# Two weight pieces over the first token half in eight banks, warm-up products, low weight parts on VectorE

## The reference, cut to what matters

```python
h = rmsnorm(x, g_mix)
z = h @ w_in                       # 1024 x 1792: lx, lg, q, k, v
lx = causal_depthwise_conv(lx, w_conv, b_conv)
y_lru = rmsnorm(rg_lru(lx, ...) * gelu(lg), g_lru_out)
y_att = rmsnorm(chunk_window_attention(q, k, v, sinks), g_attn_out)
x = x + concatenate([y_lru, y_att]) @ w_out
x = x + square(relu(rmsnorm(x, g_ffn) @ w_ff1)) @ w_ff2
x = x + sigmoid(rmsnorm(x, g_ple) @ w_ple_gate) * (p @ w_ple_proj)
return rmsnorm(x, g_final)
```

## Time and profile before

| | us |
|---|---|
| median of 3 runs (range) | 1108.56 (1108.11 to 1109.01) |
| profiled execution, its time | 1109.54 |
| its span, first to last instruction | 1107.8 |
| TensorE busy | 1073.4 (97%) |
| TensorE weight loads | 870.7 (79%) |
| VectorE busy | 726.7 (66%) |
| ScalarE busy | 419.5 (38%) |
| GpSimd busy | 472.1 (43%) |

### The profile page before, as it was taken

How to read it: one execution, slowest core, us unless ns; L and a number is a source line. 1 busy time by engine, 2 the same in 40 slices (tenths; PEclk the granted TensorE clock), 3 DMA queues, 4 the chain that set the end, 5 groups by cost and what they waited for, 6 DMA issues and landing times.

```text
span 1107.8 us, 13619 instructions
## 1 busy us (share of the span) xinstructions
PE 1073.4 (97%) x4898; PEld 870.7 (79%) x4898; DVE 726.7 (66%) x921; ACT 419.5 (38%) x725; POOL 472.1 (43%) x304
## 2 busy tenths in 40 slices
PE   6899999899999999999999999999999999999995
PEld 5778888677876888888888888888888888888895
DVE  6997666889799836536536546546545545696557
ACT  7555664454456222222222222212312312565334
POOL 2744252333306256255255355355355355293221
PEclk9999999999999999999999999999999999999998
DMA  8211102111001211211211211211111101420004
GB/s 285 77 39 38 38 1 86 39 39 39 1 1 38 76 38 38 76 38 38 76 38 38 76 38 38 76 38 40 73 38 51 63 38 61 167 76 1 1 1 153
DMA packets 20162, 61.05 MB, mean 55 GB/s; under 512 B 2080, under 2 KB 4128, under 8 KB 20128
## 3 DMA queue, kind: packets, MB, share of 16 engines
q1 hardware_dynamic: 19584, 60.08, 15.2%
q10 hardware_dynamic: 544, 0.52, 0.1%
HBM read 56.40 MB, written 4.19 MB: 55 GB/s over the span
## 4 chain that ended last, share of the span: by engine, by line
PE 79%; DVE 11%; ACT 4%; issue 3%; POOL 2%; DMA 1%; SPq 0%; DVEq 0%; ACTq 0%
PE bank L567 26%; PE bank L568 25%; PE bank L569 25%; POOL w_lo L444 1%; DVE r_mix L1288 1%; DVE lane L1335 1%; DMA stage<-in_w_in 1%; DVE acc L343 1%; POOL gx_lo L473 1%; DVE r_ffn L1288 1%; PE bank L657 1%; PE bank L615 1%; DVE xT L1682 1%; DVE h_lo L1550 1%; DVE xT L1754 1%
## 5 line engine op out<-in xcount | busy, mean ns | idle before, releaser
L567 PE MATMUL bank<-h_hi,w_hi 128*128 128x512 f32 (+1 forms) x724 | 282.6, 390 | 13.7 <-DVE h_lo L1275 9.8
L568 PE MATMUL bank<-h_lo,w_hi 128*128 128x512 f32 (+1 forms) x724 | 276.7, 382 | 0.0
L569 PE MATMUL bank<-h_hi,w_lo 128*128 128x512 f32 (+1 forms) x724 | 276.4, 382 | 0.0
L1682 DVE TENSOR_TENSOR xT<-bank,xT 128x512 f32<-128x512 f32 x256 | 173.7, 688 | 114.0 <-PE bank L569 112.3
L567 PE MATMUL bank<-u_hi,w_hi 128*128 128x512 f32 x512 | 202.2, 395 | 2.4 <-DVE xT L1682 1.1
L569 PE MATMUL bank<-u_hi,w_lo 128*128 128x512 f32 x512 | 199.4, 389 | 0.0
L568 PE MATMUL bank<-u_lo,w_hi 128*128 128x512 f32 x512 | 199.4, 389 | 0.0
L567 PEld LDWEIGHTS bank<-h_hi,w_hi 128*128 128x128 f32 x724 | 137.0, 189 | 46.6 <-issue 16.1
L521 POOL TENSOR_TENSOR w_lo<-w_raw,w_hi 128x1024 fp32r<-128x1024 f32 x30 | 78.1, 2624 | 192.2 <-ACT w_hi L1152 192.2
L568 PEld LDWEIGHTS bank<-h_lo,w_hi 128*128 128x128 f32 x724 | 137.0, 189 | 27.0 <-issue 1.9
L569 PEld LDWEIGHTS bank<-h_hi,w_lo 128*128 128x128 f32 x724 | 137.0, 189 | 26.5
(11 more groups left out here) (208 smaller groups left out, 1694.6 us busy)
## 6 DMA issues: line engine op xcount, KB each, us to landing
w_raw<-in_w_ff SPq DMA_DIRECT2D x60, 512.0 KB, 3.7
stage<-in_w_in SPq DMA_DIRECT2D x13, 512.0 KB, 3.4
stage<-in_w_out SPq DMA_DIRECT2D x8, 512.0 KB, 3.5
stage<-in_w_ple_gate SPq DMA_DIRECT2D x8, 512.0 KB, 3.9
xT<-in_x SPq DMA_DIRECT2D x7, 512.0 KB, 9.7
stage<-in_w_ff SPq DMA_DIRECT2D x4, 512.0 KB, 3.2
out_x<-xT SPq DMA_DIRECT2D x4, 512.0 KB, 2.9
out_x<-xT SPq DMA_DIRECT2D x6, 256.0 KB, 2.9
```

Source lines behind the costliest of these rows:

```text
L567: pe.matmul(o, whi, hh, start=first, stop=False, skip_group_check=onto)
L568: pe.matmul(o, whi, hl, start=False, stop=False, skip_group_check=onto)
L569: return pe.matmul(o, wlo, hh, start=False, stop=last, skip_group_check=onto)
L1682: dve.tensor_tensor(dst, bank[4 + q % 4][:, :], dst, ALU.add).then_inc(y_added, 1)
```

## The change

The first four half pieces are loaded, split and used in the order piece 0 first half, piece 1 first half, piece 0 second half, piece 1 second half (`place`). TensorE's `first_half` runs four groups (two pieces, both channel blocks) over the first half of the tokens, into banks 0 to 3; groups 4 to 7 are the same two pieces over the second half of the tokens, in banks 4 to 7 with no wait for an evacuation (`in_group`, `main_bank`). The two row sums move: the first between the third and the fourth half piece, the second into the middle of group 5. Nine products of ones with ones (`WARM`) run at the start into bank 7. Tile 0 of x is issued from ScalarE's queue. All low parts of the input projection's pieces 0 to 6 are now written by VectorE (`w_low`); GpSimd keeps the low parts of the gate inputs, the later row sums of squares and the later pieces. VectorE adds all squares of x. The gate products move to groups 8, 12, 16 and 19, and the steps tied to them with them; the row sums of the recurrent output move one group later, to 23 and 24.

```diff
-GATE_AT = [5, 9, 13, 17]
+GATE_AT = [7, 11, 15, 18]
+WARM = 9
...
             if g < L0:
-                return bank[g % IN_BANKS], g - IN_BANKS if g >= IN_BANKS else None
+                if g < 8:
+                    return bank[g], None
+                return bank[g % IN_BANKS], g - 8 if g < 12 else g - IN_BANKS
...
+        def in_group(g):
+            if g < 8:
+                return (g % 4) // 2, g // 4, g % 2
+            return g // 4, (g % 4) // 2, g % 2
+        def place(s):
+            return (s % 2, s // 2) if s < 4 else (s // 2, s % 2)
...
-            if n < IN_PIECES:
+            if n < 2:
+                eng.wait_ge(main_done, 6 + 2 * n)
+            elif n < IN_PIECES:
...
-            sp.dma_start(xT[:, 0, half(0)], x[0:P, half(0)]).then_inc(first_x_in, 16)
+            sp.dma_start(xT[:, 1, half(0)], x[P:2 * P, half(0)]).then_inc(x_in[0], 16)
             sp.dma_start(stage[:, 0, QP:HP], w_in[0, 0, :, QP:HP]).then_inc(stage_in[0], 16)
+            for s in range(1, 4):
+                load_x(s)
+                load_half(s, w_in[place(s)])
+            for i in range(4, 8):
+                load_x(i)
+            for n in range(2, IN_PIECES):
                 load_piece(n, w_in, n)
...  (GpSimd)
-            pool.wait_ge(w_split, 1)
-            low(1)
-            for i in range(2, KD):
-                add_square(pool, SS_MIX + 1, i, sq, acc)
-            low(2)
-            low(3)
...
-            for n in range(2, IN_PIECES):
-                low(2 * n)
-                low(2 * n + 1)
-                if n - 2 < LT:
-                    gate_input_low(n - 2)
...
+            for j in range(LT):
+                gate_input_low(j)
+            sums(SS_LRU, sq, acc)
+            sums(SS_LRU + 1, sq, acc)
+            pool.wait_ge(w_split, 2 * 7)
...  (TensorE)
+            def first_half():
+                pe.wait_ge(first_high, 1)
+                pe.wait_ge(h_high, H_MIX + 1)
+                (tile 0 for banks 0 and 1: high by high, then low by high, then high by low, each as its part comes)
+                for s in range(4):
+                    n, h = place(s)
+                    if s > 0:
+                        pe.wait_ge(w_split, s + 1)
+                    for k in range(4 * h + (s == 0), 4 * h + 4):
+                        if s == 0 and k == 2:
+                            pe.wait_ge(w_split, 1)
+                        if n == 0:
+                            pe.wait_ge(h_ready, H_MIX + k + 1)
+                        for m in range(2):
+                            (passes of tile k into bank[2 * n + m])
+                    if s == 2:
+                        sum_rows(SS_MIX, acc, 7)
...
-                            pe.wait_ge(rms_done, SS_MIX + 2)
+                            pe.wait_ge(main_free, 8)
...
+            for _ in range(WARM):
+                pe.matmul(bank[7][:, 0:P], ones[:, :], ones[:, :], start=True, stop=True)
...
+                if g == 5:
+                    middle = lambda: sum_rows(SS_MIX + 1, acc, 7)
+                if g == 7:
+                    pe.wait_ge(rms_done, SS_MIX + 2)
...  (ScalarE: same steps for x and the first four half pieces, in the new order)
+            act.dma_start(xT[:, 0, half(0)], x[0:P, half(0)]).then_inc(first_x_in, 16)
...
-                if g in (15, 18):
+                if g in (13, 17):
...  (VectorE)
+            mix_low(0, 0); mix_low(1, 0); (low part of half piece 0's second quarter); mix_low(2, 0)
+            (then, in this order, the sums of squares, mix_low(3..7, 0) and w_low(1), w_low(2), w_low(3) between)
             for k in range(KD):
-                split_low(H_MIX + KD + k, xT[:, k, half(1)], v_mix[:, k:k + 1], k, 1)
-                if k < 2:
-                    add_square(dve, SS_MIX + 1, k, sq, acc)
+                mix_low(k, 1)
+                add_square(dve, SS_MIX + 1, k, sq, acc)
             invert(SS_MIX, r_mix)
-            evac(0)
-            evac(1)
+            for g in range(4):
+                evac(g)
             invert(SS_MIX + 1, r_mix)
-            evac(2)
-            evac(3)
+            evac(4)
+            w_low(4)
+            w_low(5)
             conv(0)
+            evac(5)
+            evac(6)
+            evac(7)
             decay()
+            conv(1)
...
-                    states(GATE_AT.index(g - 2))
+                    j = GATE_AT.index(g - 2)
+                    if j < LT - 1:
+                        w_low(2 * (j + 3))
+                    states(j)
+                    if j < LT - 1:
+                        w_low(2 * (j + 3) + 1)
...
                 if g == 20:
                     multiply_y(2)
                     multiply_y(3)
+                    w_low(2 * 6)
+                    w_low(2 * 6 + 1)
...
-                if g == 24:
+                if g == 25:
                     norm_y(1)
```

More of the change, by code:

```diff
@@ L591, in group @@
                 last.then_inc(main_done, 1)
[L593 to L607, removed]
+            def first_half():
+                pe.wait_ge(first_high, 1)
+                pe.wait_ge(h_high, H_MIX + 1)
+                for m in range(2):
+                    pe.matmul(bank[m][:, :], w_hi[:, 0, m * P:(m + 1) * P], h_hi[:, 0, half(0)], start=True,
+                              stop=False)
+                pe.wait_ge(first_low, 1)
+                for m in range(2):
+                    pe.matmul(bank[m][:, :], w_lo[:, 0, m * P:(m + 1) * P], h_hi[:, 0, half(0)], start=False,
+                              stop=False)
+                pe.wait_ge(h_ready, H_MIX + 1)
+                for m in range(2):
+                    pe.matmul(bank[m][:, :], w_hi[:, 0, m * P:(m + 1) * P], h_lo[:, 0, half(0)], start=False,
+                              stop=False)
+                for s in range(4):
+                    n, h = place(s)
+                    if s > 0:
[5 more added lines that the diff above has]
+                            pe.wait_ge(h_ready, H_MIX + k + 1)
+                        for m in range(2):
+                            c = k * 256 + m * P
+                            last = passes(bank[2 * n + m][:, :], w_hi[:, n, c:c + P], w_lo[:, n, c:c + P],
+                                          h_hi[:, k, half(0)], h_lo[:, k, half(0)], k == 0, k == KD - 1)
+                            if k == KD - 1:
+                                last.then_inc(main_done, 1)
+                    if s == 2:
+                        sum_rows(SS_MIX, acc, 7)
@@ L704, in _ @@
                     middle = lambda: scores(g - 26)
[L705 to L709, removed]
+                group(g, n, KD, m, hf, 0, H_MIX + KD if g == 4 else None, g >= 8 and g % 4 == 0, middle)
+                if g in (23, 24):
+                    sum_rows(SS_LRU + g - 23, acc, 5)
+                if 22 <= g < 26:
+                    turn_v(g - 22)
             for u in range(UNITS):
@@ L927, in _, with mix_high, mix_square @@
             act.wait_ge(first_x_in, 16)
[L929 to L943 removed]
+            def mix_high(k, hf):
+                if (k % 2 == 0) if hf or k > 1 else (k == 1):
+                    act.wait_ge(x_in[4 * hf + k // 2], 16)
+                split_high(H_MIX + KD * hf + k, xT[:, k, half(hf)], v_mix[:, k:k + 1], k, hf)
+            def mix_square(k, hf):
+                square(KD * hf + k, sq, xT[:, k, half(hf)])
+            mix_high(0, 0)
+            mix_high(1, 0)
+            act.wait_ge(stage_in[0], 16)
+            act.activation(w_hi[:, 0, QP:HP], stage[:, 0, QP:HP], ACT.Copy).then_inc(w_high, 1)
+            mix_high(2, 0)
+            mix_square(0, 0)
+            mix_high(3, 0)
+            high(1)
+            for k in range(1, 4):
+                mix_square(k, 0)
+            mix_high(4, 0)
+            high(2)
+            mix_high(5, 0)
+            mix_square(4, 0)
+            mix_high(6, 0)
+            mix_square(5, 0)
+            mix_high(7, 0)
+            high(3)
+            mix_square(6, 0)
+            mix_square(7, 0)
+            for k in range(KD):
+                mix_high(k, 1)
+                mix_square(k, 1)
+                if k == 3:
+                    root(SS_MIX, 7, r_mix, D)
             root(SS_MIX + 1, 7, r_mix, D)
```

95 lines of the change are left out of this document (44 added, 51 removed).

## The result

The changed kernel's median is 1102.29 us (five runs, 1101.98 to 1102.64), against 1108.68 for the kernel before, measured again on the same chip: a ratio of 0.9939, 95% interval 0.9927 to 0.9951. The forecast was 1103.2. The profiled execution took 1102.33 with a span of 1100.5; the one before took 1109.54 and 1107.8.

A forecast was written before the change was run, and what follows sets the result against it. TensorE was taken as the bound; 3.4 us won at the start and 2.0 at the gates made 5.4 off the median of 1108.56, so 1103.2 us, with two in ten outside 1099.6 to 1107.0.

The forecast's parts named there:

- The start: First token half on TensorE: losses of 13.5 us fall to 10.1, 3.4 us won; group 4 at 33 to 33.5.
- Tile 1: Second tile of x, split for TensorE: ready at 10.0 us, or 10.5 if nothing is won.
- the clock was to fall behind tile 0: TensorE's products from 10.0 until 12.5 us: low clock back, costing 0.6 us.
- The bank wait: TensorE at group 4: the wait for bank 0, 1.7 us, goes because groups 4 to 7 have their own banks.
- The gates: Four gate insertions on TensorE: 0.2 us each, 0.8 in place of 2.8, so 2.0 us won.
- VectorE takes the low parts: Input projection: VectorE takes 13 half pieces at 1.2 us each, 16 us beside TensorE's work, leaving 23 idle.
- Rival 1: Input projection: VectorE becomes the bound at stretched durations, 9.9 us late in place of 0.8, giving 1112.3 us; 6%.
- Later stages: After the projection: a moved norm adds 2.7 us on VectorE before the first softmax, but nothing is lost.
- Rival 4: Attention stage gives back the 2.7 us of the moved norm, 1105.9 us; 7%.
- Rival 3: Best case: clock stays up (0.6), no gate insertion waits (0.7), low stretch at 323 goes (1.6): 1100.3 us; 16%.
- The warm-up: Nine fp32 products at TensorE's start: 3.9 us long, delaying nothing, worth 1.8 if the clock stays up, else nothing.
- signs of being right: TensorE up to 175 us: include some products at 0.43 after an early pause, and an empty gap list from 34 on.

The follow-up runs named there:

- run 4: Changed kernel with one weight piece at a time over both token halves, its second half piece still between the tiles of x: 1107.01 us, ratio 0.9982.
- run 7: Changed kernel with one weight piece at a time, the second piece's halves loaded and split after all of x: 1106.26 us, ratio 0.9975.
- run 2: Changed kernel with tile 0 of x issued from SyncE's queue, behind the vectors and ahead of tile 1: 1103.70 us, ratio 0.9951.
- run 1: Changed kernel with no warm-up products: 1102.58 us, ratio 0.9943.
- run 8: Kernel before with the nine warm-up products alone added: 1108.81 us, ratio 1.0004.
- run 10: Changed kernel with groups 4 to 7 in banks 0 to 3, each waiting for its evacuation: 1111.94 us, ratio 1.0029.
- run 5: Changed kernel with the fourth gate input's high part moved ahead of the root and gelu on ScalarE: 1100.52 us, ratio 0.9922.
- run 3: Changed kernel with GpSimd writing the low parts of pieces 2 to 6 again, in the old order: 1108.95 us, ratio 1.0002.
- run 6: Changed kernel with GpSimd writing pieces 2 to 6's low parts and the fourth gate input's high part ahead of the root: 1107.43 us, ratio 0.9990.
- run 12: Kernel before with tile 0 of x issued from ScalarE's queue: 1108.39 us, ratio 1.0000.

## Why the prediction was right, point by point

The direction and, within 0.9 us, the size were right, and so was the mechanism in the main: an earlier start, no bank wait, gates that hardly wait. That the size came so close is in part luck: the start was put 2.6 too low and the gates 1.0 too high. By the forecast's own steps:

- **The start, 3.4 forecast, 6.0 measured: a term too small.** The place of the gain was right, its size not: group 4 was to start at 33.0 to 33.5, and started at 30.40. Three parts of it were off. Tile 1 was put at 10.0 and was used at 8.06, because I let it land as late as the weight quarter of before. But the row at 8.42 has no bracket: ScalarE came to it from work of its own, so the row tells when ScalarE was free and only bounds the landing. The second piece was put at 14.6, and was there 1.8 earlier. And the clock was to fall behind tile 0 for 0.6; it stayed up, and the pauses were 0.82 and 0.63, not 1.83. Runs 4 and 7 put 4.0 to 4.7 us on the two pieces, run 2 puts 1.1 to 1.65 on the queue, run 1 at most 0.3 on the warm-up. These are not the parts of one sum: run 2 also loses clock.
  The Trainium skill ("TensorE: Matmul & The Clock Gate", "Why this matters for your kernels") warns of longer gaps only; behind 1.91 in run 8 and 1.85 in run 2 the clock fell all the same.
- **The bank wait goes: right,** and it is the largest single condition. Run 10 prices it at 9.65 us in the new order, with VectorE's queue as it is, against the 1.7 it had cost in the old: an earlier TensorE makes the same wait longer.
- **The gates, 2.0 forecast, about 1 measured.** Three insertions cost nothing (0.2 each was too much). The fourth, put at 0.2 "within a microsecond" of being late, lost 1.8. I had seen the gelu tiles ahead of it, but took GpSimd's low part at 1.2, where the two took 4.66, and did not count the two hand-overs; run 5 removes both waits and gains 1.8.
- **VectorE takes the low parts in 1.2 each and idles in between: right.** It took 1.19 to 1.23 alone and up to 2.3 beside GpSimd's work. Rival 1 fell: no product waits for VectorE's low parts. But I booked the move at what it saves on convolutions, and missed its main worth. At the new pace GpSimd's low parts would have made TensorE wait 3.8 us: at the fourth gates by stretching the decay terms on VectorE (run 3), or at group 24 by standing late in GpSimd's queue (run 6). Its worth is 6.7 to 6.9 us given the rest, and nothing of it is in the profile of before.
- **Later stages lose nothing: right.** TensorE's wait ahead of the first unit's product with the values is 1.78 before and 1.79 in the changed kernel. Rival 4 fell.
- **Rival 3** had its low stretch at 323 worth 1.6 us. It stayed, and run 1 shows that it is worth nothing, since later waits absorb it.

Start and gates together were 5.4 forecast and 7 measured in the traces; the medians show 6.4. The warm-up was right in size (4.2 us, no delay). Its worth I had left between 1.8, if the clock stays up, and nothing, if not. The clock stayed up, and it was worth 0.3 at most: run 1's slow products lie in the wait for tile 1, which would have hidden the low clock anyway. Two of my signs of being right did not come: no real product ran at 0.43 at the start, and the gap list up to 175 us has the two waits at 124.69 and 126.87.

## What to carry to other kernels

When inputs arrive one tile at a time, give the bound engine twice the work for each tile, if there are result buffers for both halves; without the buffers the same order lost more here than it won. When one engine is made earlier, go through every queue that feeds it, and every engine that those queues slow down, and ask which was only just in time: here one such step was worth as much as the gain itself, and undoing it alone took all of it. And read a load's landing only from a row whose bracket names the DMA; any other row gives a bound. Effects of parts taken out one by one don't add up, so price a wait from the kernel in which it stands.

## What the runs showed of the hardware

- **A second issuing queue brought x earlier than its issue time explains, in most kernels.** The first 8 us, first in the kernel before and then in run 12, which differs from it by the queue alone:
```profile
0.00:8.00 8.00, 0.00 (x0) 0.00 (x0) 0.94 (x4) 3.02 (x5) 0.88 (x8) 1.00 0.68 164
```
```profile
0.00:8.00 8.00, 1.53 (x4) 1.27 (x5) 3.20 (x7) 5.01 (x8) 0.88 (x8) 1.00 0.75 236
```
  The last column is GB/s. The three kernels with all loads on SyncE's queue (before, runs 2 and 8) moved 164, 184 and 192 in these 8 us. The eleven with tile 0 on ScalarE's queue moved 233 to 249, but for run 3 with 207. One issue takes 0.42; at the 398 GB/s of the earlier trace rows it is worth some 21 in these figures (an estimate). ScalarE takes tile 2 at 8.48 to 9.08 in all kernels with the second queue and at 9.75 to 10.34 in those without, but of the latter only run 2's row waits for the DMA. Each figure is of one profiled execution. Why isn't shown.
  The Trainium skill ("DMA: Bandwidth & Descriptors", "Issuing engines are not separate DMA queues") says that a second issuing engine saves only issue time. Ten of the eleven kernels speak against it; run 3 does not by itself.
- **The clock fell behind pauses of about 2 us, but not each time.** In the first 175 us products ran at 0.43 behind idle times of 1.85 to 3.82 in runs 2, 3, 4, 6, 7 and 8, and did not behind 0.63 and 0.82, nor behind 1.63 and 1.64 in runs 7 and 8, 1.76 in run 3 (at 8.65) and 1.78 in run 12. At 315 us nearly the same pause was followed by a granted clock of 0.57 in the changed kernel and 1.00 in run 1. So the pause's length alone doesn't tell what the clock will do.
- **GpSimd and VectorE stretch each other.** Two gate input low parts took GpSimd 4.66 in the changed kernel and 3.45 in run 5, where they lie beside other operations of VectorE. VectorE's 0.69 became 2.78 in run 3: it began at 115.16, behind GpSimd's subtraction of 114.89, and ended at 117.94, 0.4 behind the end of that one (half of the 5.30).
  The Trainium skill ("SBUF — State Buffer", "SBUF: two separate sides") calls the port pair that the two share an exclusive lock: of GpSimd's and certain of VectorE's instructions the one that starts first has it for its whole length. These rows agree with it.
